# Two query-key-value units of the second layer between the transposes of its normalised rows

## The reference

```python
for l in range(2):
    hx = rms_norm(x, norm1_g[l]) * (1 + sc1) + sh1        # latents
    hc = rms_norm(ctx, norm1_g[l]) * (1 + csc1) + csh1    # context
    # one projection, its columns split into head groups
    xa_b, xa_c, xa_x, xb_u, xq_g, xk_g, xv_g, xq_w, xk_w, xv_w = split_proj(hx @ w_in[l])
    ya, yb = conv_mixers(xa_b, xa_c, xa_x, xb_u, ...)      # 3 taps; 31 taps, layer norm, silu
    q_g = apply_rope(rms_norm(heads(xq_g), qn_c_g[l]), cos, sin)   # the same for k_g, q_w, k_w
    o_g = global_attn(q_g, k_g, heads(xv_g), kc_g, vc_g)
    o_w = window_attn(q_w, k_w, heads(xv_w), kc_w, vc_w, sink_d[l])
    x = x + g1 * (jnp.concatenate([ya, yb, o_g, o_w], axis=-1) @ w_out[l])
    x = x + g2 * hier_moe(rms_norm(x, norm2_g[l]) * (1 + sc2) + sh2, ...)   # top 2 of 32 experts
```

## Time and profile before

| what | value |
|---|---|
| time, median of 3 runs | 1950.57 us (1949.23 to 1951.98) |
| profiled execution, its own time | 1950.51 us |
| its span | 1948.3 us (2.2 us lie around it) |
| PE busy | 1675.0 us, 86% |
| DVE, ACT, POOL busy | 683.2, 322.7, 207.4 us |
| mean granted clock of PE | 0.955 |
| layer 1's transposes of normalised rows | from 1074.69 us |
| its ten convolution heads | from 1097.58 us |
| its first and last query-key-value unit | from 1166.35 and 1239.68 us |
| its attention, first scores | from 1252.09 us |

### The profile page before, as it was taken

How to read it: one execution, slowest core, us unless ns; L and a number is a source line. 1 busy time by engine, 2 the same in 40 slices (tenths; PEclk the granted TensorE clock), 3 DMA queues, 4 the chain that set the end, 5 groups by cost and what they waited for, 6 DMA issues and landing times.

```text
span 1948.3 us, 27000 instructions
## 1 busy us (share of the span) xinstructions
PE 1675.0 (86%) x9986; PEld 987.6 (51%) x9987; DVE 683.2 (35%) x1625; ACT 322.7 (17%) x709; POOL 207.4 (11%) x324
## 2 busy tenths in 40 slices
PE   4999998989959989999796799799959979877773
PEld 2555445754546646665353344476446635434441
DVE  1183655661442212222122577564341111111112
ACT  3110115651210000000000401364110000000000
POOL 0000000000002222222121000000002211111111
PEclk9999998999959999999998799899969999999997
DMA  9347146001239999899998621100259999999994
GB/s 381 144 195 330 64 211 259 1 1 43 116 145 426 426 426 426 340 425 426 426 426 338 268 95 79 43 1 1 82 211 426 427 426 425 426 426 426 426 424 184
DMA packets 51368, 524.56 MB, mean 269 GB/s; under 512 B 10696, under 2 KB 11368, under 8 KB 21872
## 3 DMA queue, kind: packets, MB, share of 16 engines
q1 hardware_dynamic: 33968, 481.51, 59.0%
q0 software_dynamic: 14624, 31.80, 4.3%
q10 hardware_dynamic: 2720, 10.49, 1.4%
HBM read 515.08 MB, written 25.95 MB: 278 GB/s over the span
## 4 chain that ended last, share of the span: by engine, by line
PE 62%; DMA 28%; DVE 6%; ACT 2%; issue 1%; POOL 0%; ACTq 0%; POOLq 0%; DVEq 0%
DMA ring<-in_e_down_dram 25%; PE ps L752 21%; PE ps L530 9%; PE ps L559 7%; PE ps L699 6%; PE ps L594 3%; PE ps L625 2%; PE ps L609 2%; PE ps L480 2%; PE ps L597 2%; DMA xres<-in_ctx_tokens_dram 2%; DMA r<-y_dram 1%; PE ps L740 1%; PE ps L678 1%; PE ps L489 1%
## 5 line engine op out<-in xcount | busy, mean ns | idle before, releaser
L752 PE MATMUL ps<-ring,r 128*64 128x256 f32 (+1 forms) x3920 | 534.8, 427 | 79.4 <-DMA ring<-in_e_up_dram 34.0
L752 PEld LDWEIGHTS ps<-ring,r 128*64 128x64 f32 x3920 | 310.0, 138 | 289.2 <-issue 132.7
L752 PE MATMUL ps<-r 128*64 128x256 f32 (+1 forms) x1760 | 239.9, 426 | 31.3 <-DMA r<-in_e_up_dram 14.3
L1331 DVE TENSOR_TENSOR r<-r,ps 128x128 f32<-128x128 f32 x142 | 34.5, 284 | 542.0 <-PE ps L752 542.0
L752 PEld LDWEIGHTS ps<-r 128*64 128x64 f32 x1760 | 141.3, 138 | 122.1 <-issue 55.4
L530 PE MATMUL ps<-r,ring 128*128 128x512 f32 (+1 forms) x480 | 176.5, 527 | 3.2 <-ACT r L1452 1.6
L559 PE MATMUL ps<-ring,r 128*128 128x512 f32 (+1 forms) x384 | 155.9, 560 | 0.0
L699 PE MATMUL ps<-ring,r 128*128 128x512 f32 x320 | 140.2, 594 | 2.2 <-ACT r L1602 2.2
L530 PEld LDWEIGHTS ps<-r,ring 128*128 128x128 f32 x480 | 90.9, 191 | 91.8 <-issue 86.1
L1351 DVE TENSOR_TENSOR r<-ps,r 128x512 f32<-128x512 f32 x71 | 49.1, 692 | 214.6 <-PE ps L752 214.6
L1625 ACT ACTIVATE r<-ps 128x256 f32<-128x256 f32 x71 | 27.3, 384 | 560.2 <-PE ps L752 560.2
(11 more groups left out here) (192 smaller groups left out, 1437.9 us busy)
## 6 DMA issues: line engine op xcount, KB each, us to landing
ring<-in_e_gate_dram SPq DMA_DIRECT2D x44, 2048.0 KB, 33.3
ring<-in_e_up_dram SPq DMA_DIRECT2D x44, 2048.0 KB, 35.2
ring<-in_e_down_dram SPq DMA_DIRECT2D x44, 2048.0 KB, 35.7
ring<-in_w_mod_dram SPq DMA_DIRECT2D x24, 2048.0 KB, 17.6
r<-in_e_gate_dram SPq DMA_DIRECT2D x20, 2048.0 KB, 35.9
r<-in_e_up_dram SPq DMA_DIRECT2D x20, 2048.0 KB, 38.2
r<-in_e_down_dram SPq DMA_DIRECT2D x20, 2048.0 KB, 38.4
ring<-in_w_in_dram SPq DMA_DIRECT2D x8, 2048.0 KB, 18.8
```

What stands on the lines that cost most here:

```text
L752: mm = pe.matmul(ps[g * B:(g + 1) * B, bank, 0:width], x, w[:, k, g * width:(g + 1) * width], start=(k == first), stop=(k == last), tile_p ...
```

## The change

In layer 1 the first two query-key-value units (tiles 0 and 1, group 0) leave the place behind the convolution heads. The transposes of the rows and these units now alternate on PE. Their turned-back parts, `qk_transposes`, stand behind the first two convolution heads, and DVE rotates both units ahead of `glu_product`. Their stores stay where they were. ACT copies the units in the order of the list, so ahead of the first head. Since the list decides the order of the chunks, the chunk of units 0 to 5 becomes chunk 0, and the three chunks of the convolution heads move back by one; the second half of `w_out` then waits for unit 5 and not for the fourth head. Layer 0 stays as it is.

```diff
--- before.py
+++ after.py
@@ -61,6 +61,8 @@
 
 QKV_UNITS = 2 * NT
 
+QKV_AHEAD = 2
+
 CONV_ORDER = (6, 7, 8, 9, 0, 1, 2, 3, 4, 5)
 
 
@@ -69,7 +71,7 @@
     conv = [("conv", ct) for ct in CONV_ORDER]
     qkv = [("qkv", u) for u in range(QKV_UNITS)]
     if layer:
-        return conv + qkv
+        return qkv[:QKV_AHEAD] + conv + qkv[QKV_AHEAD:]
 
     mod = [("mod", n) for n in range(12 * DEPTH)]
     steps, mod = mod[:MOD_FIRST], mod[MOD_FIRST:]
@@ -550,6 +552,9 @@
                 n = chunk_index(layer, ("qkv", u))
                 if i == 0:
                     wait_chunk(layer, n)
+                if layer and u < QKV_AHEAD:
+                    pe.wait_ge(h1_act, h1_count(layer, False) + u + 1)
+                    pe.wait_ge(h1_vec, h1_count(layer, True) + u + 1)
                 if u >= 2:
                     pe.wait_ge(qk_scaled, QKV_UNITS * layer + u - 1)
                 elif layer == 0 and u == 1:
@@ -559,7 +564,7 @@
                     mm = pe.matmul(ps[:, 4 + u % 2, c0:512], h1T[:, i, k, :], chunk_ap(layer, n)[:, k, c0:512],
                                    start=(k == 0), stop=(k == KD - 1))
                 mm.then_inc(qkv_psum, 1)
-                if u >= 1:
+                if u >= (1 + QKV_AHEAD if layer else 1):
                     qk_transposes(layer, u - 1)
 
             def ln_sums(layer, which):
@@ -810,12 +815,16 @@
                         if turned is not None:
                             mod_turn(turned)
                             turned = None
-                        if layer:
-                            h1_transposes(layer, 0, NT)
                         started = True
                     if kind == "conv":
+                        if layer and n == CONV_ORDER[0]:
+                            h1_transposes(layer, 2 * QKV_AHEAD, NT)
                         conv_projection(layer, n)
+                        if layer and CONV_AT[n] < QKV_AHEAD:
+                            qk_transposes(layer, CONV_AT[n])
                     if kind == "qkv":
+                        if layer and n < QKV_AHEAD:
+                            h1_transposes(layer, 2 * n, 2 * n + 2)
                         qkv_projection(layer, n)
                         if n in (LN_MEAN, LN_VAR):
                             ln_sums(layer, 0 if n == LN_MEAN else 1)
@@ -1382,6 +1391,9 @@
                 own(nc.vector.tensor_scalar(nsink[:, layer, :], row[:, layer, 4 * HD:4 * HD + 4], -1.0, None, ALU.mult))
                 tokens_in(layer)
                 clear_pads(layer)
+                if layer:
+                    for u in range(QKV_AHEAD):
+                        rotate(layer, u)
                 glu_product(layer)
                 for tap in range(TAPS_EARLY):
                     conv_b_tap(layer, tap)
@@ -1392,7 +1404,8 @@
                 for u in range(QKV_UNITS):
                     if layer == 0 and u == QKV_UNITS - 1:
                         mod_copy(1, MOD_CONV - 12, 12, turned_bank(MOD_CONV), 24)
-                    rotate(layer, u)
+                    if layer == 0 or u >= QKV_AHEAD:
+                        rotate(layer, u)
                     if TAPS_EARLY + u < TAPS_B:
                         conv_b_tap(layer, TAPS_EARLY + u)
                     store_qk(layer, u)
@@ -1511,7 +1524,7 @@
                 c0 = 0 if full else 256
                 h0 = 0 if full else 4
                 ac.wait_ge(qkv_psum, QKV_UNITS * layer + u + 1)
-                if u == 0:
+                if u == (QKV_AHEAD if layer else 0):
                     ac.wait_ge(conv_mul, 2 * layer + 2)
                 own(nc.scalar.copy(v_tok[:, i, group * P:(group + 1) * P], ps[:, 4 + u % 2, 384:512]))
                 if u >= 1:
```

## The result

The changed kernel takes 1942.4 us (median of 20 runs, 1939.24 to 1950.46), the kernel before beside it 1951.49 us (20 runs, 1949.23 to 1963.15). The ratio is 0.9943, with a 95% interval of 0.9928 to 0.9958: about 11 us less, 8 to 14. (The ratio is not that of the two medians, which lie 9.1 us apart. The runs fall into two groups, on which a median depends; the part on what stays open has them.) Two later timings of the same pair gave 0.9954 (0.9938 to 0.9970) and 0.9942 (0.9921 to 0.9963). The forecast was 1944.0 us against 1950.57 before, a ratio of 0.9967. The direction held, the forecast gain was too small by 2.5 to 5 us, and the cause of that is what the rest looks for.

What follows compares the result with a forecast made beforehand. PE was taken to bound layer 1 ahead of attention. 11.5 us, less 3.3 us of later start (2.0 plus 1.3 for clock) and 1.7 us for one fall, gave 6.5 us: 1950.5 to 1944.0 us, range 1940.4 to 1948.5.

Steps and rivals of the forecast that it cites:

- part 2: Layer 1's start: low clock during unit 0 costs 0.7 to 1.9 us, 1.3 taken; transposes alone had raised the clock.
- Part 4: Wider gaps before the first head and unit 3's transposes: each a bit over even chance of a 1.7 us clock fall.
- one fall is likeliest: One of the two widened gaps brings a clock fall of 1.7 us, leaving 6.5 us of gain; chance 0.39.
- Parts 1 and 3: Layer 1's transposes to unit 6: first head 2.0 us later plus clock cost, unit 6 11.5 us earlier less that delay.
- Part 5: Loads, ACT copies, added PE waits and PSUM banks cost nothing; later expert loads move forward by the whole gain.
- No fall: Neither widened gap lowers the clock: gain stays 8.2 us, time 1942.3 us; chance 0.24.
- DVE as the bound: From head 4 to unit 6, late DVE work leaves 1 to 3 us of gain, about 1948.5 us; chance 0.12.
- The cold units: Clock stays at 1.2 GHz through units 0 and 1: kernel 8.7 us slower, 1959.2 us; chance 0.05.

Runs made afterwards that it cites:

- a2_after: Changed kernel, unedited, profiled again; 120.68 us from the start of layer 1's first transposes to the start of unit 6.
- a3_after: Changed kernel, unedited, timed beside e8_second; 1942.97 us, ratio 0.9942 against the kernel before.
- b1_before: Kernel before, unedited, profiled again; 131.16 us from the start of layer 1's first transposes to the start of unit 6.
- e2: Changed kernel with only PE's part early: ACT copies and DVE rotates units 0 and 1 at their old places; ratio 1.0024 against the kernel before.
- e3: Changed kernel with four long-convolution taps moved into DVE's idle time between the products of heads 4 and 5 in layer 1; ratio 0.9955 against before.
- e5: Changed kernel with 19 idle matmuls before layer 1's first transpose group and two before the second; ratio 0.9983 against the kernel before.
- e7: Changed kernel with two extra ACT copies ahead of the last tile's modulation, lengthening the gap before the first head; ratio 0.9974 against before.
- e4: Changed kernel with one unit ahead instead of two; ratio 0.9992 against the kernel before.
- e6: Kernel before with the same idle matmuls as e5; ratio 1.0022 against the unedited kernel before.
- e8_both: Changed kernel with e3's edit, layer 1's first head waiting only for tile 4's modulation, the second for tile 5's; ratio 0.9941 against before.
- e8_second: The kernel of e8_both run again, timed beside a3_after; 1941.4 us, ratio 0.9937 against the kernel before.

## Why the prediction was right or wrong

**The table of L.** All times in us; "clock" is what unit 0 takes over 7.03 plus what a fall in one of the two gaps adds.

| kernel, profile | L | clock |
|---|---|---|
| before, the first | 129.19 | heads 68.93 |
| before, three more | 131.16, 131.10, 130.96 | heads 70.65, 70.57, 70.45 |
| changed, the first | 120.55 | 2.04 + 0 |
| changed, again | 120.66 | 2.15 + 0 |
| changed, a2_after | 120.68 | 0.48 + 1.70 |
| changed, a3_after | 120.92 | 0.72 + 1.69 |

The means are 130.6 and 120.7: 9.9 us, which is inside all three timed intervals. The forecast of 6.5 us and the 9.9 us part at three places.

**The term that was not in the sum: the clock of the kernel before, 1.4 us.** The prediction asked what the clock would cost the changed kernel and took the kernel before as it stood in one profile, with a rise 2 us ahead of the first head. In three of four profiles of the unchanged kernel the rise comes after the heads have begun, which costs 1.5 to 1.7 us in the heads and 0.3 us in T5. This is the step of the prediction that failed first: a term put at nothing because one profile did not show it. The change takes this loss away, since unit 1, T4 and T5 run at full clock right in front. The remark in part 2, that transposes alone had raised the clock, was true of that profile; in b1_before it stayed at 0.50 through T4, T5 and the first 3.5 us of matmuls. The Trainium skill, "TensorE: Matmul & The Clock Gate", section "Part 4: PE-mode transpose", says that transposes do not bring the full clock. The trace of the one execution, with the rise at 1095.5 us under T5, speaks against that as the prediction said; the three others, with rises 3.1 to 3.5 us into the heads, are nearer to what the page says.

**Part 4, the falls, 1.7 us forecast.** In the four profiles of the changed kernel two of eight gaps of 2.10 to 2.12 us brought a fall of 1.7 us, 0.85 us a run on the mean. With e2, e3, e5 and e7 it is four of thirteen such gaps. The gaps were smaller than worked out (2.12 for 2.3, 2.10 for 2.4), and the rows of the expert stage from which I took better than even odds were few: over all seventeen profiles, 30 of 59 gaps of 2.06 to 2.11 us in front of 32 matmuls of that stage brought a fall, and one of 108 gaps of 1.87 to 1.94 us. Even odds hold for that stage, then; around the heads the same gap did it in four of thirteen. The mechanism and its price were right. The odds were too high for these profiles, and "one fall is likeliest" is the term on paper that was mis-sized: 1.7 us forecast, 0.85 measured. Thirteen gaps are too few, though, to exclude even odds, so a part of this may be luck.

**Part 2, unit 0's clock, 1.3 us forecast.** Measured 2.04, 2.15, 0.48 and 0.72, mean 1.35. The mean is right, with some luck: each of the four lies outside the stated 0.7 to 1.9 us or at its edge. e5_warm shows that it is the clock.

**Parts 1 and 3, the structure, 9.5 us forecast.** At full clock it is 129.19 - (120.55 - 2.04) = 10.7 us. The heads start 1.8 us later (24.65 - 22.89) where I had 2.0. From the first head to unit 6 it takes 93.9 us where the working gives 94.8: two waits of 0.48 and 2.10 us, not 1.1 and 2.4. DVE's rounds of tap and store were mis-sized. I had taken 2.09 us for one from 1179.06 to 1181.15, which held a wait of DVE for PE's transposes; where nothing is waited for, a round takes 1.86 us:

```profile
1180.26 1.41 DVE L1004 SCALAR_TENSOR_TENSOR r<-r,small 128x512 f32<-128x512 f32 x2
...
1182.12 1.41 DVE L1004 SCALAR_TENSOR_TENSOR r<-r,small 128x512 f32<-128x512 f32 x2
...
1183.97 0.55 DVE L1020 TENSOR_REDUCE qk_sum<-r 128x6 f32<-128x384 f32 x1
```

Two rounds are 3.71 us, from 1180.26 to 1183.97. e3_taps confirms that these rounds are what PE waits for.

**Part 5** held: the loads landed, no table was loaded again, no new wait stands behind unit 6. The sum with its corrections is 6.5 + 1.4 (before) + 0.85 (falls) + 1.2 (structure) - 0.05 (unit 0) = 9.9 us.

**The rivals.** "No fall" (8.2 us) was the nearest, and two of the four profiles of the changed kernel had none. DVE as the bound is refuted as a loss, though DVE does set the two waits. The cold units are refuted in every profile of the changed kernel: unit 1 took 7.03 us in all of them.

**What stays open.** The timed gains (11.1, 9.0 and 11.3 us by the three ratios) lie on both sides of 9.9, too coarse to say more. One reason is that the timed runs fall into groups. Divided at their widest step, the changed kernel's first twenty are eleven of 1939.24 to 1942.62 us and nine of 1945.20 to 1950.46, the twenty beside it of before fifteen of 1949.23 to 1954.24 and five of 1959.03 to 1963.15. The medians of the two lower groups are 1941.11 and 1950.70 us, 9.6 us apart, close to the 9.9 of L. A median or ratio of all runs depends also on how many fall into the upper group.

The profiles show one source of such a difference, in layer 1's attention, which no kernel here changes. From unit 6 to the end twelve profiles have 744.0 to 746.5 us and five (e2, e4, e6, e7, e8_both) 750.0 to 751.4. In the stretch from 140 to 150 us behind unit 6 the granted clock was 0.66 in each of the five and 1.00 in each of the twelve. The same matmuls behind the same gap, first in the first profile of the kernel before, then in e6_before_warm:

```profile
1345.50 1.09 PE L625 MATMUL ps<-r 128*64 128x128 f32 x16 [0.68 <-ACT r L1569]
```

```profile
1350.57 1.97 PE L632 MATMUL ps<-r 128*64 128x128 f32 x16 [0.68 <-ACT r L1576]
```

The gap ahead of that one was 1.31 us in both. Of the 6.8 us between these two profiles from unit 6 on, 2.7 come with this fall, 1.0 ahead of it and the rest behind it. Among the five is e8_both but not e8_second, which is the same kernel: 5.4 us lie between them behind unit 6, more than the 3 us that the version gains in L, and six runs of each cannot resolve that. Why the clock falls there in some executions only is not found. Nor is it shown whether a change makes the fall more or less frequent. So it is open, too, whether the 4 to 6 us by which e5_warm and e6_before_warm were timed slower are the idle matmuls' own. The profile of e6_before_warm has this fall; that of e5_warm doesn't and was the shortest of its runs, 1941.09 us, while eight of its eleven were 1947.01 us or more.

## What to carry to other kernels

Idle time of one engine is only worth filling if the engines that finish the work have room at the same place: the early matmuls alone lost, and with the copies and rotations moved as well they gained the whole 10 us. Where a short stretch follows idle time, its cost depends on where the clock stands, and that differs between executions of the same kernel; take several profiles of the kernel before as well as of the changed one, compare a local interval and not the span, look at whether the timed runs form one group or two before a median is trusted, and ask of the old kernel too which losses its one profile happens not to show.

## What the runs showed of the hardware

The same sequence of transposes with the same gaps raised PE's clock before the first head in one profile of the unchanged kernel and not in three others, where it rose 3.1 to 3.5 us after the first head's start. Of 108 gaps of 1.87 to 1.94 us in the expert stages of all profiles one brought the clock down, of 59 gaps of 2.06 to 2.11 us 30 did; gaps of 2.1 us around the heads did in 4 of 13 cases, and the two of 3.41 and 4.09 us both did. Each such fall cost 1.7 us (5.36 for 3.67, 8.83 for 7.13); behind the gap of 4.09 us it cost 2.9. The fall can come when PE is already at work again, 1.3 us after the gap in e5_warm. Shorter gaps do not exclude one: in the attention, behind gaps of 1.3 and 0.7 us with 0.6 us of transposes between them, the clock fell in 5 of 17 profiles.
